# Moving weight rounding to ScalarE, splitting the S5 output stage and re-spacing fill work in a hybrid decoder layer

## The reference, cut to what matters

```
h = rms_norm(x, norm_mix)
proj = h @ w_in            # NSA q, three k/v sets, gates | S5 input | stick-breaking q,k,v | three merge gates
o_a = nsa_mixer(...)       # compressed blocks (softmax, also picks the top-k blocks), selected blocks, sliding window
o_b = s5_mixer(...)        # complex diagonal state space, y = Re(C x) + D u, GELU, then y * sigmoid(y @ w_glu)
o_c = stick_breaking(...)  # strictly causal, weight = sigmoid(z) * product of sigmoid(-z) of the later keys
merged = sum_b sigmoid(gate_b) * (o_b @ w_branch_b)
x = x + merged @ w_out
x = x + conv_ffn(rms_norm(x, norm_ffn))
```

## Time and profile before

| | |
|---|---|
| median of 3 runs | 1465.17 us |
| the profiled execution: own time | 1466.77 us |
| its span, first to last instruction | 1465.0 us |
| PE busy | 1400.4 us (96%) |
| DVE busy | 712.1 us (49%) |
| ACT busy | 366.6 us (25%) |
| POOL busy | 469.5 us (32%) |
| mean granted TensorE clock | 0.977 |

### The profile page before, as it was taken

The page is one execution under the profiler, slowest core; times in us unless marked ns, Lnnn a source line. Parts: engine busy times, 40 slices in busy tenths (PEclk is TensorE's granted clock), DMA queues, the critical chain, the costliest instruction groups (busy, mean ns, idle before and its releaser), DMA issues.

```text
span 1465.0 us, 18556 instructions
## 1 busy us (share of the span) xinstructions
PE 1400.4 (96%) x7421; PEld 1122.1 (77%) x7421; DVE 712.1 (49%) x1187; ACT 366.6 (25%) x720; POOL 469.5 (32%) x237
## 2 busy tenths in 40 slices
PE   5998799999999889999899999999999999999998
PEld 4887467799887666666688888788888888888887
DVE  5898665534543675666545231632322322464641
ACT  5311544400111145444411110521111111132110
POOL 4324002134713110011134343243433434444442
PEclk9999899999989899999999999999999999999999
DMA  7420101032102000000011141411111111141122
GB/s 184 46 53 19 44 1 30 15 77 55 37 18 55 19 19 1 19 19 19 19 33 40 43 158 58 144 47 54 43 55 45 43 57 43 43 172 43 45 78 94
DMA packets 126823, 76.46 MB, mean 52 GB/s; under 512 B 39312, under 2 KB 113424, under 8 KB 126736
## 3 DMA queue, kind: packets, MB, share of 16 engines
q1 hardware_dynamic: 126752, 75.46, 18.4%
HBM read 66.93 MB, written 8.52 MB: 52 GB/s over the span
## 4 chain that ended last, share of the span: by engine, by line
PE 84%; DVE 11%; ACT 3%; issue 2%; DMA 0%; SPq 0%; DVEq 0%; ACTq 0%
PE ps L669 23%; PE ps L670 23%; PE ps L671 23%; PE ps L1142 3%; PE ps L1175 2%; PE ps L1159 2%; PE ps L904 1%; PE ps L921 1%; PE ps L934 1%; PE ps L684 1%; PE ps L1100 1%; DVE merged L1803 1%; DVE small L1993 1%; ACT arena L1286 1%; PE ps L878 1%
## 5 line engine op out<-in xcount | busy, mean ns | idle before, releaser
L580 POOL TENSOR_TENSOR wh<-raw,zero 128x1024 fp32r<-128x1024 f32 (+2 forms) x92 | 186.0, 2022 | 938.0 <-PE ps L671 919.7
L669 PE MATMUL ps<-hTh,wh 128*128 128x512 f32 x1008 | 404.0, 401 | 0.8 <-ACT arena L1316 0.8
L671 PE MATMUL ps<-hTh,wl 128*128 128x512 f32 x1008 | 396.6, 393 | 0.0
L670 PE MATMUL ps<-hTl,wh 128*128 128x512 f32 x1008 | 396.4, 393 | 0.0
L583 POOL TENSOR_TENSOR wl<-raw,wh 128x1024 fp32r<-128x1024 f32 (+2 forms) x93 | 257.7, 2771 | 32.3 <-ACT wh L1322 25.1
L669 PEld LDWEIGHTS ps<-hTh,wh 128*128 128x128 f32 x1008 | 192.0, 190 | 45.5 <-issue 7.1
L671 PEld LDWEIGHTS ps<-hTh,wl 128*128 128x128 f32 x1008 | 191.6, 190 | 40.9
L670 PEld LDWEIGHTS ps<-hTl,wh 128*128 128x128 f32 x1008 | 192.2, 191 | 37.9
L671 PE MATMUL ps<-wh,hTl 128*128 128x512 f32 (+2 forms) x512 | 179.1, 350 | 0.0
L670 PE MATMUL ps<-wl,hTh 128*128 128x512 f32 (+2 forms) x512 | 179.0, 350 | 0.0
L669 PE MATMUL ps<-wh,hTh 128*128 128x512 f32 (+2 forms) x512 | 179.0, 350 | 0.0
(11 more groups left out here) (331 smaller groups left out, 1659.8 us busy)
## 6 DMA issues: line engine op xcount, KB each, us to landing
raw<-in_w_in SPq DMA_DIRECT2D x35, 512.0 KB, 3.9
raw<-in_w_up SPq DMA_DIRECT2D x32, 512.0 KB, 4.0
raw<-in_w_down SPq DMA_DIRECT2D x16, 512.0 KB, 3.7
merged<-in_x SPq DMA_DIRECT2D x8, 512.0 KB, 7.4
raw<-in_w_out SPq DMA_DIRECT2D x8, 512.0 KB, 3.6
merged<-in_x SPq DMA_DIRECT2D x2, 2048.0 KB, 10.4
x_keep<-merged SPq DMA_DIRECT2D x2, 2048.0 KB, 11.0
conv<-x_keep SPq DMA_DIRECT2D x1, 2048.0 KB, 8.6
```

The lines of the kernel that those rows point to most:

```text
L580: eng.tensor_tensor(wh[:, p, 0:n], raw[:, p, 0:n], zero1[:, 0:1].broadcast_to((P, n)), ALU.add).then_inc(s_hi[0], 1)
L669: mm(out_, ah, bh, start=first, stop=False, skip_group_check=True)
L670: mm(out_, ah, bl, start=False, stop=False, skip_group_check=True)
L671: return mm(out_, al, bh, start=False, stop=last, skip_group_check=True)
```

## The change

- `HIGH_ON_ACT` takes in panels 2 to 8: ACT writes their high parts, at given places between its evacuations; POOL writes only the low parts.
- `s5_outputs` is split: the lag part stays in step 0, the state part goes to step 1; `y_evac` goes from step 1 to step 2.
- `glu` is split by output column block: one half in step 6, one in step 8, both in banks 6 and 7. Its sigmoids are in steps 7 and 9, `s5_glu` in steps 8 and 10.
- Fill pieces begin in step 5. Steps 5 to 12 have one piece each, the eight gate pieces of the first panel. The other 32 are dealt over steps 13 to 23; step 13 has pieces 8 and 9 of the first panel.
- In `PLAN`, fills 48 to 51 go ahead of `("pc", 4)`; the six fills ahead of `("mk", 1)` become two. Fill 49 is piece 9 of its panel, fill 44 is its piece 8.

```diff
-HIGH_ON_ACT = [P_SBMERGE + 1]
+HIGH_ON_ACT = [*range(2, 9), P_SBMERGE + 1]
...
-        FILL0 = 8
-        SB_FILLS = [(q, k) for q in range(4) for k in (0, 1, 2, 3, 8, 4, 5, 6, 7, 9)]
+        FILL0 = 5
+        SB_FILLS = [(q, k) for q in range(4) for k in (range(10) if q == 0 else (0, 1, 2, 3, 8, 4, 5, 6, 7, 9))]
         def sb_fills(j):
             if j < FILL0 or j >= NJ:
                 return []
-            n, w = len(SB_FILLS), NJ - FILL0
-            return SB_FILLS[n * (j - FILL0) // w:n * (j + 1 - FILL0) // w]
+            if j < FILL0 + 8:
+                return SB_FILLS[j - FILL0:j - FILL0 + 1]
+            rest = SB_FILLS[8:]
+            n, w, i = len(rest), NJ - FILL0 - 8, j - FILL0 - 8
+            return rest[n * i // w:n * (i + 1) // w]
...
-        PLAN += fills[40:42] + [("mk", 0), ("pvc", 3)] + fills[42:44] + [("half", 1)] + fills[44:48]
+        PLAN += fills[40:42] + [("mk", 0), ("pvc", 3)] + fills[42:44] + [("half", 1)] + fills[44:52]
         PLAN += [("pc", 4), ("pc", 5), ("pvc", 4), ("pc", 6), ("pvc", 5), ("pc", 7), ("pvc", 6), ("pvc", 7)]
-        PLAN += fills[48:54] + [("mk", 1)]
+        PLAN += fills[52:54] + [("mk", 1)]
         PLAN += fills[54:58]
...
-            def s5_outputs():
+            def s5_lags():
                 eng.wait_ge(S("toep_in"), 16 * S5_CHUNK)
-                eng.wait_ge(S("c_pow"), 1)
                 eng.wait_ge(S("v_read"), 2)
...
+            def s5_states():
+                eng.wait_ge(S("c_pow"), 1)
                 for hf in range(2):
                     eng.wait_ge(S("x_ready"), hf + 1)
...
-            def glu():
+            def glu(oc):
                 eng.wait_ge(S("wglu_in"), 16)
-                for k in range(4):
-                    oc, hf = k // 2, k % 2
+                for hf in range(2):
                     eng.wait_ge(S("yg_ready"), 2)
+                    if oc:
+                        eng.wait_ge(S("glu_sig"), hf + 1)
                     for kc in range(2):
-                        ins = mm(ps[:, 4 + k, :], wglu[:, kc * 256 + oc * P:kc * 256 + (oc + 1) * P],
+                        ins = mm(ps[:, 6 + hf, :], wglu[:, kc * 256 + oc * P:kc * 256 + (oc + 1) * P],
...
                 if j == 0:
-                    s5_outputs()
+                    s5_lags()
+                if j == 1:
+                    s5_states()
                 if j == S5_Y:
                     y_transposes()
-                if j == S5_GLU:
-                    glu()
+                if j in (S5_GLU, S5_GLU + 2):
+                    glu((j - S5_GLU) // 2)
...
             evac(1)
+            panel_high(2)
             eng.wait_ge(S("s5_angles"), 1)
...
             evac(3)
+            panel_high(3)
             evac(4)
             evac(5)
+            panel_high(4)
...
-            for m in range(10, 16):
+            evac(10)
+            evac(11)
+            panel_high(7)
+            panel_high(8)
+            for m in range(12, 16):
                 evac(m)
...
-                if j == S5_GLU + 1:
-                    for k in range(4):
+                if j in (S5_GLU + 1, S5_GLU + 3):
+                    for hf in range(2):
+                        k = j - S5_GLU - 1 + hf
                         eng.wait_ge(S("glu_ps"), k + 1)
-                        eng.activation(gl[k], ps[:, 4 + k, :], ACT.Sigmoid).then_inc(S("glu_sig"), 1)
+                        eng.activation(gl[k], ps[:, 6 + hf, :], ACT.Sigmoid).then_inc(S("glu_sig"), 1)
...
-                if j == 1:
+                if j == 2:
                     y_evac()
                 if j == S5_Y + 1:
                     y_skip()
-                if j == S5_GLU + 2:
-                    s5_glu()
+                if j in (S5_GLU + 2, S5_GLU + 4):
+                    s5_glu((j - S5_GLU) // 2 - 1)
```

More of the change, by code:

```diff
@@ L362, in gate_prod @@
         def gate_prod(q, hf):
-            return 2 * hf + 1 if q < 4 or 8 <= q < 16 else hf + 1
+            return 2 * hf + 1 if 0 < q < 4 or 8 <= q < 16 else hf + 1
         def branch_prod(q, hf):
-            return 2 * hf + 2 if q < 4 or 8 <= q < 16 else hf + 3
+            return 2 * hf + 2 if 0 < q < 4 or 8 <= q < 16 else hf + 3
         PLAN = fills[0:4] + [("q", n) for n in range(TB)] + fills[4:14] + [("cs", 0), ("cs", 1), ("half", 0)] + fills[14:22]
         PLAN += [("split", 0)] + fills[22:40] + [("pc", 0), ("pc", 1), ("pvc", 0), ("pc", 2), ("pvc", 1), ("pc", 3), ("pvc", 2)]
-        PLAN += fills[40:42] + [("mk", 0), ("pvc", 3)] + fills[42:44] + [("half", 1)] + fills[44:48]
+        PLAN += fills[40:42] + [("mk", 0), ("pvc", 3)] + fills[42:44] + [("half", 1)] + fills[44:52]
         PLAN += [("pc", 4), ("pc", 5), ("pvc", 4), ("pc", 6), ("pvc", 5), ("pc", 7), ("pvc", 6), ("pvc", 7)]
-        PLAN += fills[48:54] + [("mk", 1)]
+        PLAN += fills[52:54] + [("mk", 1)]
         PLAN += fills[54:58]
@@ L947, in sb_fill @@
                         if q == 0:
-                            eng.wait_ge(S("glu_sig"), 4)
+                            eng.wait_ge(S("y_read"), 4)
                         else:
@@ L1342, in _ @@
             evac(7)
+            panel_high(5)
             for b in range(4):
@@ L1348, in _ @@
             evac(9)
+            panel_high(6)
             eng.wait_ge(S("lag_ps"), 1)
@@ L1774, in y_skip, with s5_glu @@
                         ALU.mult, ALU.add).then_inc(S("y_read"), 1)
-            def s5_glu():
-                for k in range(4):
-                    oc, hf = k // 2, k % 2
+            def s5_glu(oc):
+                for hf in range(2):
+                    k = 2 * oc + hf
                     t = slice(hf * HALF, (hf + 1) * HALF)
@@ L1786, in s5_glu @@
                         ins.then_inc(S("br_ready"), 1)
-                then(eng.tensor_copy(mixT[:, 0, 0:HALF], qS[:, 0, 0:HALF]))
+                if oc:
+                    then(eng.tensor_copy(mixT[:, 0, 0:HALF], qS[:, 0, 0:HALF]))
             def merge(q, halves=(0, 1)):
```

## The result

The changed kernel takes 1454.57 us (median of 6 runs, 1451.38 to 1457.46); the kernel before, timed beside it, 1466.43 us. The ratio is 0.9911, with an interval of 0.9885 to 0.9938: 0.9% faster. That is 11.9 us less than the median beside it and 10.6 less than the 1465.17 that the prediction started from, where 4.0 were forecast. The time lies 0.4 us under the range. Executions of the kernel before come in two groups, a lower one (1463.7 to 1469.8 us) and an upper one (1473.3 to 1477.3 us), and the ratios in this document count both.

What follows compares the result with a forecast made beforehand. PE, busy 1400 of 1465 us, was taken as the bound, leaving only its waits and half-clock time to win. Terms -4.2 - 1.2 - 0.1 + 1.5 = -4.0 gave 1461.2 us, range 1455.0 to 1467.5.

Steps and rivals of the forecast that it cites:

- step 1, by the table load: PE's wait ahead of step 1's scores: 2.0 us left, with ACT's table load as the new limit.
- step 13, merge of piece 8: Piece 9 in step 13 waits for DVE to merge piece 8: a new PE wait, +2.8 us.
- fill 49, merge of fill 44: In NSA, fill 49 waits for a merge queued behind the block choice: PE stands 7.8 us instead of 5.1, +2.7.
- The DVE chain: S5 chain on DVE ahead of step 1: freed from POOL's high parts, it ends between 129 and 134 us, from 139.8.
- POOL's hold on the first scan: POOL's low part of panel 9, until 138.6 us, holds the first DVE scan; covered by the lag part of S5.
- clock term of the moved fills: NSA stretch, 489 to 503 us: two clock falls cost 2.0 and 1.7 us instead of 4.7 lost, -1.0 us.
- term of -5.4: Rounding of panels 2 to 8 on ScalarE: -4.2 us of wait before step 1 and -1.2 of clock behind it.
- term of -0.1 for the S5 parts: S5 in parts and fill work from step 5: gains and new waits sum to -0.1 us, ends -5 and +4.
- Less clock is lost: Rival: PE's waits of 2.0, 3.2 and 2.8 us no longer lower the clock; -8.6, to 1456.6 us; chance 0.22.
- Thin steps lose the clock: Rival: many short PE waits in steps 2 to 12 bring repeated clock falls; 1468 to 1470 us; chance 0.12.
- Full price: Rival: clock falls at the 2.0 us wait and NSA's second fall stays as long; 1464.2 us; chance 0.20.
- The rounding doesn't do what it says: Rival: DVE's chain isn't shorter, low parts meet other operations; step 1 stays at 140.6, 1466.6 us; chance 0.04.

Runs made afterwards that it cites:

- table_early: The changed kernel with a sigmoid of 8 elements on ScalarE ahead of ACT's last four evacuations, so the table loads earlier: 1452.96 us, ratio 0.9872.
- plan_only: The kernel before with only the four fills moved ahead of the NSA transposes: 1461.3 us, ratio 0.9947.
- act_only: The kernel before with only the rounding of panels 2 to 8 moved to ScalarE: 1461.3 us median, ratio 0.9951.
- merge_first: The changed kernel with fill 44 ahead of the block choice and fills 45 to 53 ahead of the transposes: 1455.35 us, ratio 0.9904.
- both_waits: table_early with the branch products of the first two panels placed so that neither meets an unfinished merge: 1456.17 us, ratio 0.9916.

## Why the prediction was wrong

**What held.** The waits, one by one, with their places and causes:

| wait | forecast | measured |
|---|---|---|
| step 1, by the table load | 2.0 | 2.16 |
| steps 5 to 7, GELU | 1.9 + 2.6 - 1.4 = 3.1 | 0.48 + 3.31 |
| behind the GLU sigmoids | 0.4 | 0.43 |
| steps 8 to 12 | 0.9 + 0.7 | 0.73 + 0.67 |
| step 13, merge of piece 8 | 2.8 | 2.81 |
| fill 49, merge of fill 44 | 7.8 | 7.54 |

The waits as a whole fell by 2.2 us instead of the 0.6 forecast: the fill piece beside the GELU saved 0.7 instead of 1.4, and small waits that I had not counted went. The DVE chain ended 12.5 us sooner, a little more than the 5.6 to 10.3 I had reckoned, and that changed nothing, since the table load was the limit. POOL's hold on the first scan was there (2.78 us instead of 0.74) and was covered. The small waits that went are 0.37, 0.72 and 0.47 us before the scores and products of three steps, and 0.6 of the NSA products instead of 0.2. Taking the load out of the path took 1.28 us off the wait in table_early. The Trainium skill ("ScalarE: Activation LUTs", What ACT_TABLE_LOAD costs) adds a drain and prices the load at 2.66 us, which is more than the whole wait of 2.16; the measurement decides for 1.28.

**What failed: the clock term of the moved fills.** The prediction had +2.7 of waiting and -1.0 of clock there. The wait was +2.4 and -0.6 behind it. The clock is where it went wrong: I expected two falls, as before, the second a little shorter, and priced nothing behind 503 us. In eight of eleven profiles the second (3.3 us, at 496 to 503) did not come, and the falls at 540 and 591 were absent in six of eleven, where the seven profiles without the edit all have them. By the means of the table that is -4.6 us of clock instead of -1.0 (-3.8 to -8.1 like with like), and with +1.8 of waits -2.8; timed directly, -3.1 to -5.3. That turns +1.5 into about -4, and 4.0 + 5.5 is 9.5 us: the mean distance of the changed kernel from the lower group of before is 1465.7 - 1455.8 = 9.9.

**What was off by chance of the profile.** The median of 1454.57 owes about 1 us to the six executions that were drawn: thirteen have a mean of 1455.8. And the kernel before was read from an execution with a fall at 90 us, so that I valued the rounding against a wait of 6.3 where 9.5 is usual. Its term of -5.4 was not confirmed either: -3.6 and -2.7 in two of its three comparisons, -8.8 in the third. The term of -0.1 for the S5 parts lies among -0.9, -3.2 and +2.9. That these two and the rest add up to the distance above is partly luck.

**What the prediction could not see.** It took a spread of 2.7 us from three executions. Over 97 the kernel before has 41 in the upper group, 9.2 us above the lower. None of the 13 executions of the changed kernel (up to 1459.9 us), of the 13 of plan_only (up to 1465.2) and of the 12 of act_only (up to 1468.3) reaches it. Over all executions the change is therefore worth 1469.6 - 1455.8 = 13.8 us, and the moved fills alone 7.8.

**The rivals.** *Less clock is lost* (1456.6) came nearest, but for another reason than it gave: the falls behind the waits of 2.2 and 3.3 us did come in the first profile after (2.8 and 1.7 us at 133 and 167), and those that stayed away were further on. *Thin steps lose the clock* is excluded: 140 to 163 and 171 to 380 us have no fall in the first profile after, and in the two further ones steps 2 to 12 have only the fall at 165 or 168, behind the GELU wait. *Full price* has its waits right and its clock wrong. *The rounding doesn't do what it says* is excluded by the chain's end at 127.24.

**What stays open.** Which of two executions of one program has a fall at 540 is not explained by any wait; the counts (7 of 7 against 5 of 11, a split that chance alone gives in one of 40 draws) make it likely that the order of fills matters, and don't say how. In the changed kernel itself the two falls came in two profiles of three, so their absence is no property of it; the fall behind the transposes is what went more regularly. Whether removed waits are paid back by the clock isn't settled either: merge_first and both_waits lost 2.9 and 3.7 us of waiting against the changed kernel and none of the time, with clock sums of 23.4 and 24.3, but the changed kernel's own three sums are 19.0, 24.8 and 23.8. No profile shows an execution of the upper group of before, so what sets it apart, and why the changed kernels have none, is open beyond its granted clock of 0.970 against 0.978.

## What to carry to other kernels

Split a span into waits, clock loss and the rest before you size anything: here the rest was constant to 1.3 us either way, the six waits of the table were forecast to 0.7 us each, and the clock loss varied by 6 us between executions of one program. Take clock terms from several profiles, and the spread of the kernel before from more than three executions. In this kernel dense work ahead of small matmuls with waits between them was worth more than its waits said; whether it is elsewhere has to be measured. A wait behind one engine that is lengthened by another can grow when its predecessor gets faster, so read the wait in more than one execution before it is priced.

## What was not expected of the hardware

- DVE's scans are held by POOL's rounding too: eight of them took 7.35 us beside POOL and 2.63 without it. A fall of the clock at 90 us, 40 us earlier, decided which operations were met.
- Two groups of executions of one kernel lie 9.2 us apart (1465.7 and 1474.9 us in the mean) at granted clocks of 0.978 and 0.970. That difference times 1465 us is 11 to 12 us, as an estimate: the clock can cover the whole distance. The waits of the upper group are in no profile.
- The commonest fall costs 1.6 to 1.8 us of time (some 3.4 us of PE's work at half clock): about 90 of some 170 in the eighteen profiles. The length of the wait in front doesn't set the price: in the first profile after, 1.8 us were lost around the wait of 7.5, 1.7 behind that of 3.3, and 2.8 around that of 2.2. In table_early one began at 133.5 us beside waits of 0.78 and 0.88 us; in both_waits, with the same two waits, there was none there.
